# A 64x64-cell scan: another order of the work on four engines, and A copied out of PSUM into a tile of its own

## What is computed

```python
def wkv_scan(state, r, w, k, v, a, b, reverse):
    def step(s, inp):
        r_t, w_t, k_t, v_t, a_t, b_t = inp
        sa = jnp.einsum('bhij,bhj->bhi', s, a_t)
        s = s * w_t[:, :, None, :] + sa[..., None] * b_t[:, :, None, :] + v_t[..., None] * k_t[:, :, None, :]
        return s, jnp.einsum('bhij,bhj->bhi', s, r_t)
...
    for n, rev in enumerate((False, True)):
        s_ctx, yc = run_scan(state0, fc, n, rev)
        _, yl = run_scan(s_ctx, fl, n, rev)
        y_lat = y_lat + yl
```

## Time and profile before

| | |
|---|---|
| Time, median of 3 runs | 2223.35 us (2222.14 to 2228.94) |
| The profiled execution, its own time | 2223.72 us |
| Its span, first to last instruction | 2221.9 us |
| Mean granted clock of TensorE | 0.982 |
| PE busy over the span | 2041.6 us, 92% |
| PEld busy | 1325.2 us, 60% |
| DVE busy | 1130.4 us, 51% |
| ACT busy | 646.0 us, 29% |
| GpSimd busy | 539.7 us, 24% |

### The profile page before, as it was taken

The page is one execution under the profiler, slowest core; times in us unless marked ns, Lnnn a source line. Parts: engine busy times, 40 slices in busy tenths (PEclk is TensorE's granted clock), DMA queues, the critical chain, the costliest instruction groups (busy, mean ns, idle before and its releaser), DMA issues. The chain is left out here.

```text
span 2221.9 us, 64762 instructions
## 1 busy us (share of the span) xinstructions
PE 2041.6 (92%) x28556; PEld 1325.2 (60%) x28556; DVE 1130.4 (51%) x2187; ACT 646.0 (29%) x1825; POOL 539.7 (24%) x669
## 2 busy tenths in 40 slices
PE   7999999999999999999896888888988898889698
PEld 3556565355444455544344777787878787878443
DVE  5443343134946670042624665665666666656574
ACT  4111111134255532210012332333333333333332
POOL 1010010023032410011122333333433333333011
PEclk9999999999999999999997999999999999999899
DMA  9201002701127765555413233523333323232732
GB/s 354 81 20 38 19 19 107 291 29 38 32 76 205 192 174 182 176 165 190 144 64 109 72 95 97 141 71 94 80 84 82 90 75 94 73 91 61 235 119 109
DMA packets 269818, 248.23 MB, mean 112 GB/s; under 512 B 92769, under 2 KB 226145, under 8 KB 266082
## 3 DMA queue, kind: packets, MB, share of 16 engines
q1 hardware_dynamic: 269538, 244.09, 36.0%
HBM read 164.32 MB, written 79.69 MB: 110 GB/s over the span
## 5 line engine op out<-in xcount | busy, mean ns | idle before, releaser
L2168 PE MATMUL ps<-M,NG 64*64 64x64 f32 x6400 | 258.3, 222 | 44.0 <-DVE M L2046 42.7
L1019 PE MATMUL ps<-xt,w_slab 128*128 128x512 f32 (+1 forms) x800 | 297.5, 525 | 0.0
L2168 PEld LDWEIGHTS ps<-M,NG 64*64 64x64 f32 x6400 | 221.9, 136 | 60.8 <-DVE M L2046 54.3
L1019 PEld LDWEIGHTS ps<-xt,w_slab 128*128 128x128 f32 x800 | 148.3, 190 | 146.3 <-issue 122.6
L2168 PE MATMUL ps<-TT,MT 64*64 64x64 f32 x5120 | 209.9, 220 | 5.9 <-issue 3.4
L2168 PEld LDWEIGHTS ps<-TT,MT 64*64 64x64 f32 x5120 | 179.4, 135 | 16.4 <-issue 6.4
L1895 POOL TENSOR_TENSOR SP<-S,decay 128x128 f32<-128x128 f32 x152 | 61.2, 403 | 518.8 <-DVE S L2080 503.4
L2071 DVE STREAM_TRANSPOSE MT<-M 128x256 f32<-128x256 f32 x240 | 106.0, 442 | 147.9 <-ACT M L1958 147.9
L1958 ACT ACTIVATE M<-ps 128x128 f32<-128x128 f32 x240 | 66.6, 278 | 353.7 <-PE ps L2168 353.7
L2029 DVE COPY_PREDICATED TT<-mask,ps 128x128 f32<-128x128 int32 x400 | 123.5, 309 | 54.5 <-PE ps L2168 45.0
L645 PE MATMUL ps<-h,fgo 128*128 128x512 f32 x320 | 141.6, 597 | 2.4 <-PEq L202 2.4
(11 more groups left out here) (298 smaller groups left out, 3996.7 us busy)
## 6 DMA issues: line engine op xcount, KB each, us to landing
feat<-feature_scratch SPq DMA_DIRECT2D x160, 256.0 KB
feature_scratch<-k_feats SPq DMA_DIRECT2D x64, 320.0 KB, 5.2
feature_scratch<-k_feats SPq DMA_DIRECT2D x24, 640.0 KB, 6.9
k_feats<-in_modw SPq DMA_DIRECT2D x8, 1536.0 KB, 6.6
w_slab<-in_rwin SPq DMA_DIRECT2D x24, 512.0 KB, 6.7
V<-v_token_scratch SPq DMA_DIRECT2D x320, 32.0 KB, 2.6
fgo<-in_modw SPq DMA_DIRECT2D x8, 1024.0 KB, 9.2
fw_slab<-in_fwin SPq DMA_DIRECT2D x16, 512.0 KB, 4.5
```

The source lines that it names most:

```text
L1019: mm = pe.matmul(ps[:, bank, 0:n], (w1t if i is None else w[:, i % 2])[:, k, :], src[:, k, a:a + n], start=k == 0, stop=k == KT - 1)
L2168: mm = pe.matmul(out[o, b, :], L[o, b, :], R[o, b, :], start=True, stop=True)
```

## The change

ACT now copies A into a new tile `AT` (two buffers, 128x256, flat), and b into `NG` in a second operation. `first_mt1` and the t levels read `AT`. GpSimd does SP1 between the operands, and the operand that A is made of comes last. PE, ACT and DVE get another order of the same work:

- PE: p0 is moved ahead of m4, r_state0 behind m4, p1 ahead of b_state0, y0 behind m8, y1 behind t32.
- ACT: R0, n0, copy of m4, SA0, exponentials, n1, m8, y0, R1, SA1, m16, m2, y1, xt.
- DVE: sums, x0, r0, mt4, t8, state0, mt1, m1, mt8, t16, t2, x1, mt16, r1, state1, t32, mt2, t4.

```diff
-AA = {"n0": 1, "n1": 2, "m2": 3}
+AA = {"n0": 2, "n1": 4, "m2": 5}
...
-DA = {"x0": 1, "x1": 2, "mt1": 3, "m1": 4, "t2": 5, "mt2": 6, "t4": 7}
+DA = {"x0": 1, "mt1": 2, "m1": 3, "t2": 4, "x1": 5, "mt2": 6, "t4": 7}
...
+    AT = [sb(f"AT{s}", [P, B4, CK]) for s in two]
...
-                g.tensor_tensor(d4(ar[l][:, :, 0, :]), fe(every, 384, 256), before(cc, every), ALU.mult).then_inc(op_ready, 1)
+                if is_lat(cc):
+                    g.tensor_tensor(d4(ar[l][:, :, 2, :]), fe(every, 512, 640), upto(cc, every), ALU.mult).then_inc(op_ready, 1)
                 g.tensor_tensor(d4(ar[l][:, :, 1, :]), d4(ident.unsqueeze(1).broadcast_to([P, B4, CK])),
                                 pend(cc, every).unsqueeze(3).broadcast_to([P, 2, 2, CK]), ALU.mult).then_inc(op_ready, 1)
-                if is_lat(cc):
-                    g.tensor_tensor(d4(ar[l][:, :, 2, :]), fe(every, 512, 640), upto(cc, every), ALU.mult).then_inc(op_ready, 1)
+
+            def last_operand(j, cc):
+                s, l = par(cc), lng(cc)
+                every = slice(0, P)
+                g.tensor_tensor(d4(ar[l][:, :, 0, :]), F[s][:, 384:896].rearrange("p (d x) -> p d x", d=2)[:, :, 0:P].rearrange("p d (b t) -> p d b t", b=2), before(cc, every), ALU.mult).then_inc(op_ready, 1)
...
                 if c >= 0:
                     state_scaled(j, c, 0)
-                    if c < NCH - 1:
-                        state_scaled(j, c, 1)
-                if ahead or c + 3 < NCH:
+                if coming:
                     operands(j, c + 3)
+                if 0 <= c < NCH - 1:
+                    state_scaled(j, c, 1)
+                if coming:
+                    last_operand(j, c + 3)
...
-                act.activation(gout(NG[lng(cc)], d, 0, 2), gall(0, 0, 2), ACT.Copy).then_inc(aa, 1)
+                act.activation(AT[par(cc)][:, 2 * d:2 * d + 2, :], gall(0, 0, 1), ACT.Copy).then_inc(aa, 1)
+                act.activation(gout(NG[lng(cc)], d, 1, 2), gall(0, 1, 2), ACT.Copy).then_inc(aa, 1)
...
-                v.copy_predicated(MT1[s][:], mask[:, 0:256].rearrange("p (b t) -> p b t", b=B4), NG[lng(cc)][:, :, 0, :]).then_inc(da, 1)
+                v.copy_predicated(flat(MT1[s][:]), mask[:, 0:256], flat(AT[s][:])).then_inc(da, 1)
...
-                level(lev(5), NG[lng(cc)][:, :, 0, :], M[s], pb)
+                level(lev(5), AT[s], M[s], pb)
```

More of the change, by code:

```diff
@@ L1682 @@
 PB = {"m4": 1, "t8": 2, "m8": 3, "t16": 4, "m16": 5, "t32": 6, "mt32": 7}
-AA = {"n0": 1, "n1": 2, "m2": 3}
+AA = {"n0": 2, "n1": 4, "m2": 5}
 AB = {"m4": 1, "m8": 2, "m16": 3, "xt": 4}
-DA = {"x0": 1, "x1": 2, "mt1": 3, "m1": 4, "t2": 5, "mt2": 6, "t4": 7}
+DA = {"x0": 1, "mt1": 2, "m1": 3, "t2": 4, "x1": 5, "mt2": 6, "t4": 7}
 DB = {"mt4": 1, "t8": 2, "mt8": 3, "t16": 4, "mt16": 5, "t32": 6}
 LAT_ONLY = lambda n: [0, 0] + [n] * (NCH - 2)
-PER = {"first": [len(PA)] * NCH, "second": [len(PB)] * NCH, "act_first": [len(AA)] * NCH, "act_second": [len(AB)] * NCH,
+PER = {"first": [len(PA)] * NCH, "second": [len(PB)] * NCH, "act_first": [AA["m2"]] * NCH, "act_second": [len(AB)] * NCH,
        "dve_first": [len(DA)] * NCH, "dve_second": [len(DB)] * NCH, "two": [2] * NCH,
@@ L1905, in operands @@
                 chunk_done(g, j, cc - SETS)
-                g.tensor_tensor(d4(ar[l][:, :, 0, :]), fe(every, 384, 256), before(cc, every), ALU.mult).then_inc(op_ready, 1)
+                if is_lat(cc):
+                    g.tensor_tensor(d4(ar[l][:, :, 2, :]), fe(every, 512, 640), upto(cc, every), ALU.mult).then_inc(op_ready, 1)
                 g.tensor_tensor(d4(ar[l][:, :, 1, :]), d4(ident.unsqueeze(1).broadcast_to([P, B4, CK])),
                                 pend(cc, every).unsqueeze(3).broadcast_to([P, 2, 2, CK]), ALU.mult).then_inc(op_ready, 1)
-                if is_lat(cc):
-                    g.tensor_tensor(d4(ar[l][:, :, 2, :]), fe(every, 512, 640), upto(cc, every), ALU.mult).then_inc(op_ready, 1)
+            def last_operand(j, cc):
+                s, l = par(cc), lng(cc)
+                every = slice(0, P)
+                g.tensor_tensor(d4(ar[l][:, :, 0, :]), F[s][:, 384:896].rearrange("p (d x) -> p d x", d=2)[:, :, 0:P].rearrange("p d (b t) -> p d b t", b=2), before(cc, every), ALU.mult).then_inc(op_ready, 1)
             def period(j, c, ahead):
+                coming = ahead or c + 3 < NCH
                 if c >= 0:
                     state_scaled(j, c, 0)
-                    if c < NCH - 1:
-                        state_scaled(j, c, 1)
-                if ahead or c + 3 < NCH:
+                if coming:
                     operands(j, c + 3)
+                if 0 <= c < NCH - 1:
+                    state_scaled(j, c, 1)
+                if coming:
+                    last_operand(j, c + 3)
             for j in range(KT):
@@ L1975, in period @@
                 A_, B_, Q_ = c + 2 >= 0 and (ahead or c + 2 < NCH), c + 1 >= 0 and (ahead or c + 1 < NCH), c >= 0
+                if Q_:
+                    r(j, c, 0)
+                if A_:
+                    first_n(j, c + 2, 0)
                 if B_:
@@ L1978, in period @@
                 if Q_:
-                    r(j, c, 0)
+                    sa(j, c, 0)
                 if ahead or c + 3 < NCH:
@@ L1984, in period @@
                 if A_:
-                    first_n(j, c + 2, 0)
-                if Q_:
-                    sa(j, c, 0)
+                    first_n(j, c + 2, 1)
                 if B_:
                     second(j, c + 1, "m8")
-                if A_:
-                    first_n(j, c + 2, 1)
                 if Q_ and is_lat(c):
@@ L1995, in period @@
                     r(j, c, 1)
+                    sa(j, c, 1)
                 if B_:
                     second(j, c + 1, "m16")
-                if Q_:
-                    sa(j, c, 1)
                 if A_:
@@ L2087, in period @@
                     masks()
+                if A_:
+                    first_x(j, c + 2, 0)
+                if A_ and is_lat(c + 2):
+                    first_r(j, c + 2, 0)
                 if B_:
                     second_mt(j, c + 1, 4)
[L2090 to L2094, removed]
                     second_t(j, c + 1, 8)
@@ L2097, in period @@
                     state(j, c, 0)
-                if B_:
-                    second_mt(j, c + 1, 8)
                 if A_:
-                    first_x(j, c + 2, 1)
                     first_mt1(j, c + 2)
@@ L2104, in period @@
                 if B_:
+                    second_mt(j, c + 1, 8)
                     second_t(j, c + 1, 16)
                 if A_:
-                    if is_lat(c + 2):
-                        first_r(j, c + 2, 1)
                     first_t(j, c + 2, 2)
+                    first_x(j, c + 2, 1)
+                if B_:
+                    second_mt(j, c + 1, 16)
+                if A_ and is_lat(c + 2):
+                    first_r(j, c + 2, 1)
                 if Q_:
@@ L2112, in period @@
                 if B_:
-                    second_mt(j, c + 1, 16)
+                    second_t(j, c + 1, 32)
                 if A_:
                     first_mt2(j, c + 2)
-                if B_:
-                    second_t(j, c + 1, 32)
-                if A_:
                     first_t(j, c + 2, 4)
@@ L2174, in t2 @@
                 ge(pe, da, count("dve_first", j, cc - 1, DA["t4"]))
-                level(lev(4), NG[lng(cc)][:, :, 0, :], M[s], pa)
+                level(lev(4), AT[s], M[s], pa)
             def m2(j, cc):
@@ L2316, in period @@
                     a_state(j, c, 0)
-                    r_state(j, c, 0)
+                if A_:
+                    products(j, a, 0)
                 if B_:
                     m4(j, b)
-                if A_:
-                    products(j, a, 0)
                 if Q_:
+                    r_state(j, c, 0)
                     sa(j, c, 0)
@@ L2325, in period @@
                     t(j, b, 8)
+                if A_:
+                    products(j, a, 1)
                 if Q_:
                     b_state(j, c, 0)
+                if B_:
+                    m(j, b, 8)
                 if lat:
                     y(j, c, 0)
[L2330 to L2333, removed]
                 if Q_:
@@ L2346, in period @@
                     b_state(j, c, 1)
-                if lat:
-                    y(j, c, 1)
                 if A_:
@@ L2352, in period @@
                     t(j, b, 32)
+                if lat:
+                    y(j, c, 1)
                 if A_:
```

## The result

The changed kernel takes 2158.19 us (median of 4 runs, 2155.26 to 2162.05), 0.9702 of before, with a 95% interval from 0.9674 to 0.9729: 3.0% faster. The forecast was faster by 6.6%, 2077.5 us in a range from 2040 to 2135. The profiled execution took 2158.71 us, 65.0 less than that of before.

A forecast was written before the change was run, and what follows sets the result against it. TensorE's weight loads, waiting mainly for ACT and DVE copies, bound the kernel. Waits of 2.65 us become 0.46, period 8.65; with issue 0.1 and clashes up to 0.15, 8.9: 77 × 1.9 = 146 off 2223.7 gives 2077.5 us, range 2040 to 2135.

The forecast's parts named there:

- issue, 7.3 us over 80 periods or 0.1: TensorE's weight loads: waits with no releaser but issue, added to the 8.65 us period as 0.1 us.
- The walk: One period followed through all engines' queues: 2.65 us of waits become 0.46, so the period is 8.65 us.
- the bound that I gave on the gain: Nothing left but TensorE's work: 80 × 2.6 = 208 us gained, giving 2015 us.
- The waits of `b_state` for SA, of t2 for M and of sa0 for R: TensorE load waits: SA and R waits go; t2's for M falls from 0.5 us to 0.2 per period.
- MT1 ends 0.31 us behind GpSimd's product: DVE's masked copy: before, 0.31 us behind GpSimd's product; the forecast has it end 0.44 behind, near 4.94 in the period.
- Waits of t8 for m4's copy: TensorE's level t8 was to wait for ACT's copy of m4, a new wait of 0.17 us per period.
- loads busy over 90%: Sign in the profile after: TensorE's weight loads busy over 90% of the scan.
- The split: A and b copied separately on ACT: about 0.34 us per period, hidden; 27 us if not covered.
- `AT` at nothing for MT1: Flat input alone for DVE's masked copy: costed at no gain, bounds 0 and 0.2 us per period.
- The DMA queue: Rival: SyncE's feature loads behind the y store become the bound; 2109 us, up to 2132, chance 0.14.
- The DVE queue: Rival: MT1 waits for one more GpSimd product, delaying later masks; 9.6 us per period, 2131 us, chance 0.08.
- SP1 delayed nothing: Rival: GpSimd's SP1, now behind the operands, holds up `state` 1; slower, 2248 us at 7.2, chance 0.03.

The follow-up runs named there:

- e5: Changed kernel with each level product made of 4 matmuls of 128 moving columns instead of 8 of 64: 2047.9 us, 0.9207 of before.
- e8: Kernel before, in its own order, with A copied into the flat tile and b in a second copy: 2229.4 us, 1.0018 of before.
- e7: Changed kernel with A left in NG, one copy per direction, MT1 and levels reading NG: 2167.1 us, 0.9742 of before.
- e11: Changed kernel with four already satisfied semaphore waits added on TensorE at level products, 1600 instructions in all: 2236.8 us, 1.0052 of before.

## Why the prediction was wrong

**The step that failed** is "To this comes issue, 7.3 us over 80 periods or 0.1". It was the smallest term of the sum and measured 106 us, 1.3 a period; 8.65 + 1.3 is the 10.0 that was found. I took as a constant what is a wait like any other: it showed 7.3 us because the other waits covered it. While TensorE waited 0.78 us for SA and 0.5 for M, the next block arrived, 2.2 us ahead of its first instruction in the mean. With those waits gone, the blocks became the chain of the period. The trace of before held what was needed: 226 packets for the instructions of the program, a longest issue wait of 1.3 us, and 610 instructions in 10.8 us, that is one block every 4.5 us. The walk asked for one every 3.6. That no block comes so often was not to be read from a mean, but it was worth a rival, and there was none; the bound that I gave on the gain was TensorE's work alone.

**The walk itself held, as far as the runs can tell.** The waits of `b_state` for SA, of t2 for M and of sa0 for R went, as it had them (147 us of named waits before, under 7 after). One tenth of the periods of the changed kernel take 9.03 us or less by ACT's copy `xt`, and with fewer instructions the mean is 8.6. How exact the 8.65 is stays open, since e5's levels are shorter too. One reading in it doesn't fit its row: MT1 ends 0.31 us behind GpSimd's product, and the walk gives it 0.44 behind that, so MT1 came 0.1 late in the sum. "Waits of t8 for m4's copy" are small: all waits of the levels for ACT's M are 4.3 us, and the walk had 0.17 a period, 14 us, for t8 alone; "loads busy over 90%" came out as 84%.

**The split** was costed at nothing for ACT, and `AT` at nothing for MT1. MT1's 0.444 bears out the second. For the first, e8 lost 4 us in the old order, and e7 without the split is 9 us slower than the changed kernel: small either way.

**The rivals.** The DMA queue as I put it, with DVE's sums waiting for features, is worth 5.4 us in 4 waits. But DMA traffic mattered by a way that no rival named, through the instruction blocks, 44 us. The DVE queue did not take the waits over, and SP1 delayed nothing.

**What stays open.** What the way from a block's start to its fetch consists of: why data traffic lengthens it (1.58 with features, 1.34 without), why added instructions do (1.85 in e11), and why spreading the loads doesn't shorten it. Runs with less y traffic were not tried. A direct count of instructions at the same work was not reached: e5 changes the work a little, e11 costs time of its own.

## What to carry to other kernels

When an engine's waits are to be removed, ask what comes next for the engine itself: divide its instructions by the size of a block and see how often a block would have to come. Here a block of 256 instructions of TensorE came every 3.9 to 4.1 us in the mean where blocks were the bound. A level product of 8 matmuls in fp32 is 16 loads and 16 matmuls in the trace and takes 0.46 us, so eight of them would use up a block in 3.7. An "issue" wait that is small today can be hidden behind other waits. Where it is the bound, fewer and wider instructions pay: the same edit gave 110 us here, of which up to 56 are shorter work, and 25 in the order that waits for semaphores.

## What the runs showed of the hardware

- TensorE's instructions come in blocks of 16,384 bytes, 256 instructions. Where they were the bound (changed kernel), the next fetch began 1.58 us in the mean after a block was entered, 1.06 in the quickest twentieth; it took 1.12, and the first instruction followed 1.4 us after its end.
- Leaving out 640 KB of loads per period sped the kernel up by 44 us, though no instruction of TensorE waited for them by name; with the same loads, 10 us in the order whose TensorE waited for semaphores.
- 1600 instructions that only wait on semaphores satisfied long before cost 78 us in one order and 110 in the other, 49 and 69 ns each with what they bring.
